# Norm and rotary turn of queries and keys inside the product stage, evictions on ScalarE

## The reference, cut to what matters

```python
def rms_norm(x, g):
    xf = x.astype(jnp.float32)
    y = xf * lax.rsqrt(jnp.mean(xf * xf, axis=-1, keepdims=True) + NORM_EPS)
    return (y * g.astype(jnp.float32)).astype(x.dtype)

def rope_rotate(u, ang):
    u1, u2 = jnp.split(u, 2, axis=-1)
    cs = jnp.cos(ang).astype(u.dtype)
    sn = jnp.sin(ang).astype(u.dtype)
    return jnp.concatenate([u1 * cs - u2 * sn, u2 * cs + u1 * sn], axis=-1)

def axial_rope(x, ang_r, ang_c):
    xr, xc = jnp.split(x, 2, axis=-1)
    ...
    return jnp.concatenate([rope_rotate(xr, ar), rope_rotate(xc, ac)], axis=-1)

def diff_qkv(pq, pk, pv, qn_g, kn_g):
    B, L, _ = pq.shape
    q = rms_norm(pq.reshape(B, L, DIFF_HEADS, 2, DIFF_HEAD_DIM), qn_g)
    k = rms_norm(pk.reshape(B, L, DIFF_HEADS, 2, DIFF_HEAD_DIM), kn_g)
    v = pv.reshape(B, L, DIFF_HEADS, DIFF_V_DIM)
    return q, k, v
```

## Time and profile before

| | before |
|---|---|
| median of 3 runs | 4459.89 us |
| the profiled execution | 4462.74 us, its span 4460.9 us |
| TensorE, VectorE, ScalarE busy | 81%, 38%, 20% of the span |
| product stage of the attention branch | from 682 to 811 us of the span |
| `head_norms` and `rope` stages | 811 to 856 us |
| `transposes` stage | 856 to 864 us |

### The profile page before, as it was taken

One profiled execution on the slowest core, in us unless ns is written; L12 is line 12 of the kernel. 1 busy time (PEld: TensorE's weight loads), 2 busy tenths in 40 slices (PEclk: granted clock), 3 DMA queues, 4 the chain that ended last, 5 costly groups with the idle time before them and its releaser, 6 DMA issues. The chain is left out here.

```text
span 4460.9 us, 68948 instructions
## 1 busy us (share of the span) xinstructions
PE 3593.8 (81%) x29742; PEld 2797.0 (63%) x29742; DVE 1713.9 (38%) x3137; ACT 881.6 (20%) x1426; POOL 58.1 (1%) x74
## 2 busy tenths in 40 slices
PE   4979979579973777747899767999899589778887
PEld 2768968457553433326648557888788555656676
DVE  3645543642232000025444364444300542343433
ACT  2135421132011111111111322111000213221211
POOL 0000000000000000000000000000000000000000
PEclk7979989789985999978899888999999799887888
DMA  5130016113422999963411001444410110112122
GB/s 208 52 120 4 4 50 179 41 46 99 132 85 101 422 422 422 422 239 111 134 43 62 16 10 53 114 113 115 121 52 1 33 36 1 34 57 66 57 76 76
DMA packets 379413, 494.21 MB, mean 111 GB/s; under 512 B 15994, under 2 KB 325787, under 8 KB 370436
## 3 DMA queue, kind: packets, MB, share of 16 engines
q1 hardware_dynamic: 369588, 456.12, 29.4%
q0 software_dynamic: 4432, 25.70, 1.5%
q10 hardware_dynamic: 5120, 8.39, 0.5%
HBM read 458.70 MB, written 31.47 MB: 110 GB/s over the span
## 5 line engine op out<-in xcount | busy, mean ns | idle before, releaser
L288 PE MATMUL banks<-leading,w_rest 128*128 128x512 f32 (+2 forms) x1920 | 726.7, 378 | 128.0 <-DVE w_rest L248 128.0
L288 PE MATMUL banks<-rest,w_leading 128*128 128x512 f32 (+2 forms) x1920 | 714.1, 372 | 0.0
L288 PE MATMUL banks<-leading,w_leading 128*128 128x512 f32 (+2 forms) x1920 | 710.4, 370 | 0.0
L288 PEld LDWEIGHTS banks<-leading,w_rest 128*128 128x128 f32 (+1 forms) x1920 | 380.6, 198 | 201.6 <-issue 85.8
L288 PE MATMUL banks<-w_rest,leading 128*128 128x256 f32 (+3 forms) x1332 | 395.4, 297 | 61.9 <-DVE w_rest L248 61.9
L248 DVE TENSOR_TENSOR w_rest<-land,w_leading 128x1024 fp32r<-128x1024 f32 (+3 forms) x296 | 280.0, 987 | 402.2 <-ACT w_leading L242 402.2
L288 PEld LDWEIGHTS banks<-leading,w_leading 128*128 128x128 f32 (+1 forms) x1920 | 380.2, 198 | 64.1
L288 PEld LDWEIGHTS banks<-rest,w_leading 128*128 128x128 f32 (+1 forms) x1920 | 381.2, 199 | 59.9
L242 ACT CAST w_leading<-land 128x1024 fp32r<-128x1024 f32 (+3 forms) x296 | 239.0, 855 | 779.9 <-DMA land<-in_w_in 314.8
L288 PE MATMUL banks<-w_leading,rest 128*128 128x256 f32 (+3 forms) x1332 | 391.2, 294 | 0.0
L288 PE MATMUL banks<-w_leading,leading 128*128 128x256 f32 (+3 forms) x1332 | 390.8, 293 | 0.0
(11 more groups left out here) (532 smaller groups left out, 4787.5 us busy)
## 6 DMA issues: line engine op xcount, KB each, us to landing
wg<-in_w_exp_gate SPq DMA_DIRECT2D x32, 2048.0 KB, 28.4
wu<-in_w_exp_up SPq DMA_DIRECT2D x32, 2048.0 KB, 28.4
wd<-in_w_exp_down SPq DMA_DIRECT2D x32, 2048.0 KB, 27.9
ws<-in_ada_w SPq DMA_DIRECT2D x96, 512.0 KB, 3.9
land<-in_w_in SPq DMA_DIRECT2D x41, 1024.0 KB, 5.9
land<-in_ffn_up SPq DMA_DIRECT2D x44, 512.0 KB, 5.3
land<-in_ffn_up SPq DMA_DIRECT2D x88, 256.0 KB, 3.3
ws<-in_w_ada SPq DMA_DIRECT2D x32, 512.0 KB, 3.9
```

The lines of the kernel that those rows point to most:

```text
L288: mm = nc.tensor.matmul(bank_of(r, kind, at), lhsT, rhs, start=(k == 0 and q == 0), stop=(k == kt - 1 and q == len(each) - 1))
```

## The change

`products` gets two hooks, `after_dve` and `after_act`, called on VectorE and ScalarE after each result. In the attention branch the evictions go to ScalarE (`nc.scalar.copy`), the banks of the results are 6 in place of 4, and the two stages `head_norms` and `rope` are gone. Their work is done by VectorE in the hook, tile by tile (512 elements per partition), from result 8 on: after results 8 and 9 the squares and sums of the query tiles, two tiles each; at 10 the mean; at 12 the reciprocal; at 12, 14, 16, 18 the two multiplications of the norm, at 13, 15, 17, 19 the turn of the same tile. At 20, 21, 22 the squares and sums of the keys, at 23 the mean, at 25 the reciprocal; at 25 to 30 one key tile each, tiles 0 and 1 (context) with the norm alone, tiles 2 to 5 with norm and turn. ScalarE takes the two square roots after its evictions of results 11 and 24. Squares, sums and swapped halves use the buffer of `qT`, which is free until the transposes.

```diff
--- before.py
+++ after.py
@@ -151,7 +151,7 @@
     m.ahead_next += 1

 
-def products(nc, m, jobs, xT, evac, evac_on, banks=4, kt=KD, wslots=WSLOTS, beside=None, width=512, split=False, k_chunks=1, side=(), pooled=None):
+def products(nc, m, jobs, xT, evac, evac_on, banks=4, kt=KD, wslots=WSLOTS, beside=None, width=512, split=False, k_chunks=1, side=(), pooled=None, after_dve=None, after_act=None):

 

@@ -337,6 +337,16 @@
                     if t:
                         side_add(dve, t - 1)

+            def read_act(act, r, count, j, kind, at):
+                read(act, r, count, j, kind, at)
+                if after_act is not None:
+                    after_act(act, r)
+
+            def read_dve(dve, r, count, j, kind, at):
+                read_both(dve, r, count, j, kind, at)
+                if after_dve is not None:
+                    after_dve(dve, r, read_sem)
+
             def follow(eng, r, count, j, kind, at):
                 if beside is not None:
                     beside(eng, r, j, at, read_sem, aux_sem)
@@ -348,13 +358,13 @@

             @block.scalar
             def _(act):
-                each_result(act, round_weights, read if evac_on == "scalar" else follow)
+                each_result(act, round_weights, read_act if evac_on == "scalar" else follow)

             @block.vector
             def _(dve):
                 if side:
                     nc.vector.tensor_copy(m.cond_wide[:, :, 0:2], side[0][1]).then_inc(spread_sem, 1)
-                each_result(dve, part_weights, read_both)
+                each_result(dve, part_weights, read_dve)
                 if side:
                     side_add(dve, len(side) - 1)

@@ -874,13 +884,87 @@

             def evac(out, j, at, chain):
                 dst = (m.q, m.k, m.v)[j // 2][:, at[0] - (NTC if j < 2 else 0), 256 * (j % 2):256 * (j % 2 + 1)]
-                return nc.vector.tensor_copy(dst, out)
-
-            products(nc, m, jobs, hT_of(m), evac, "vector", split=True, width=256, side=modulation_tiles(m, a, 0, 16, 48))
-            head_norms(nc, m, [(m.q[:].rearrange("p t (n e) -> p (t n) e", e=HD), m.qk_gain[:, 0:HD]),
-                               (m.k[:].rearrange("p t (n e) -> p (t n) e", e=HD), m.qk_gain[:, HD:2 * HD])], HD, EPS)
-            heads = lambda x, t: x[:, t, :].rearrange("p (n e) -> p n e", e=HD)
-            rope(nc, m, [(heads(m.q, t), 8, t) for t in range(NTL)] + [(heads(m.k, NTC + t), 8, t) for t in range(NTL)])
+                return nc.scalar.copy(dst, out)
+
+            heads = lambda x: x.rearrange("p (n e) -> p n e", e=HD)
+            spare = m.qT[:, :, :].rearrange("p a b -> p (a b)")
+            squares, swapped = heads(spare[:, 0:512]), heads(spare[:, 512:1024])
+            sums, roots, rstd = spare[:, 1024:1104], spare[:, 1104:1184], spare[:, 1184:1264]
+            after_q, after_k = 2 * NTL, 2 * NTL + 2 * NT
+            step_sem, summed_sem, rooted_sem = [nc.alloc_semaphore(x) for x in ("qk_step", "qk_summed", "qk_rooted")]
+
+            def after_act(act, r):
+
+                for which, at in ((0, after_q + 3), (1, after_k + 4)):
+                    if r == at:
+                        act.wait_ge(summed_sem, which + 1)
+                        o, n = ((0, 8 * NTL), (8 * NTL, 8 * NT))[which]
+                        nc.scalar.activation(roots[:, o:o + n], sums[:, o:o + n], ACT.Sqrt).then_inc(rooted_sem, 1)
+
+            counted = [0]
+
+            def after_dve(dve, r, read_sem):
+
+                def step(ins):
+                    counted[0] += 1
+                    ins.then_inc(step_sem, 1)
+                    dve.wait_ge(step_sem, counted[0])
+
+                def square_sums(x, t, first):
+                    step(nc.vector.tensor_tensor(squares, heads(x[:, t, :]), heads(x[:, t, :]), ALU.mult))
+                    step(nc.vector.tensor_reduce(sums[:, first + 8 * t:first + 8 * t + 8], squares, AX, ALU.add))
+
+                def mean(first, n):
+                    nc.vector.tensor_scalar(sums[:, first:first + n], sums[:, first:first + n], 1.0 / HD, EPS, ALU.mult, ALU.add).then_inc(summed_sem, 1)
+
+                def inverse(first, n, which):
+                    dve.wait_ge(rooted_sem, which)
+                    step(nc.vector.reciprocal(rstd[:, first:first + n], roots[:, first:first + n]))
+
+                def scale(x, t, first, gain):
+                    h = heads(x[:, t, :])
+                    step(nc.vector.tensor_tensor(h, h, bc(rstd[:, first + 8 * t:first + 8 * t + 8].unsqueeze(2), HD), ALU.mult))
+                    step(nc.vector.tensor_tensor(h, h, gain.unsqueeze(1).to_broadcast([P, 8, HD]), ALU.mult))
+
+                def turn(x, t, row):
+                    h = heads(x[:, t, :])
+                    xv, sw = h.rearrange("p n (a h e) -> p n a h e", a=2, h=2), swapped.rearrange("p n (a h e) -> p n a h e", a=2, h=2)
+                    sn = m.rope_sin[:, row, :].rearrange("p (a h e) -> p a h e", a=2, h=2)
+                    for s in range(2):
+                        step(nc.vector.tensor_tensor(sw[:, :, :, s, :], xv[:, :, :, 1 - s, :], sn[:, :, s, :].unsqueeze(1).to_broadcast([P, 8, 2, 16]), ALU.mult))
+                    step(nc.vector.tensor_tensor(h, h, m.rope_cos[:, row, :].unsqueeze(1).to_broadcast([P, 8, HD]), ALU.mult))
+                    step(nc.vector.tensor_tensor(h, h, swapped, ALU.add))
+
+                n = r - after_q
+                if 0 <= n < 2:
+                    dve.wait_ge(read_sem, after_q)
+                    square_sums(m.q, 2 * n, 0)
+                    square_sums(m.q, 2 * n + 1, 0)
+                if n == 2:
+                    mean(0, 8 * NTL)
+                if n == 4:
+                    inverse(0, 8 * NTL, 1)
+                if 4 <= n < 12 and n % 2 == 0:
+                    scale(m.q, (n - 4) // 2, 0, m.qk_gain[:, 0:HD])
+                if 4 <= n < 12 and n % 2 == 1:
+                    turn(m.q, (n - 4) // 2, (n - 4) // 2)
+                n = r - after_k
+                if 0 <= n < 3:
+                    dve.wait_ge(read_sem, after_k)
+                    square_sums(m.k, 2 * n, 8 * NTL)
+                    square_sums(m.k, 2 * n + 1, 8 * NTL)
+                if n == 3:
+                    mean(8 * NTL, 8 * NT)
+                if n == 5:
+                    inverse(8 * NTL, 8 * NT, 2)
+                if 5 <= n < 5 + NT:
+                    t = n - 5
+                    scale(m.k, t, 8 * NTL, m.qk_gain[:, HD:2 * HD])
+                    if t >= NTC:
+                        turn(m.k, t, t - NTC)
+
+            products(nc, m, jobs, hT_of(m), evac, "scalar", split=True, width=256, side=modulation_tiles(m, a, 0, 16, 48), banks=6,
+                     after_dve=after_dve, after_act=after_act)
             transposes(nc, m, [([m.q[:, t, h * P:(h + 1) * P] for h in range(4)], m.qT[:, :, t * P:(t + 1) * P], None, None) for t in range(NTL)]
                        + [([m.k[:, t, h * P:(h + 1) * P] for h in range(4)], m.kT[:, :, t * P:(t + 1) * P], None, None) for t in range(NT)])
         (m.att,) = buffers(nc, ctx, att=[NTL, 512])
```

## The result

The changed kernel takes 4401.76 us (median of 4 runs, 4393.08 to 4404.5), the kernel before 4459.26 us in the same comparison (4439.4 to 4460.54). The ratio is 0.9878, 95% interval 0.9847 to 0.9909. That is 57.5 us less, where 43.6 us were forecast and 4411 to 4424 us was the range. The profiled execution took 4399.98 us (span 4397.8), against 4462.74 us (span 4460.9): 62.8 us less.

What follows compares the result with a forecast made beforehand. TensorE was taken to bound the product stage and VectorE the norm and turn stages behind it. 44.70 - 1.55 + 0.5 = 43.6 us off 4459.89 gave 4416.3 us, range 4411 to 4424.

Steps and rivals of the forecast that it cites:

- What goes: Between product stage and transposes: the norm and turn stages vanish, so transposes start 44.70 us sooner.
- The lag at result 31: End of product stage: VectorE overruns the rhythm at results 27 to 30, so the stage ends 1.55 us later.
- the lower bound: Lag at result 31: 1.2 us if the addition overlaps its copy, against 2.0 us at the other end.
- Behind the parting: Result 23, after VectorE parts weights: a lag of 1.82 us, gone by result 24.
- TensorE does not wait: Product stage: VectorE may be 2.65 us late, greatest lag 1.82, so TensorE never waits, 0.8 us to spare.
- ScalarE: Product stage: 32 added evictions of 0.37 to 0.42 us, later casts and square roots cost nothing, hidden under matmuls.
- The transposes: Transposes after the product stage: start at the low clock again, perhaps for less long, gaining 0.5 us.
- the most to be gained: First 16 transposes: at most 1.2 us, from 3.65 to the 2.46 us that VectorE's copies need.
- The sum for the place: Product stage to scores: removed stages less the lag plus the transposes' gain, 43.6 us in all.
- The rest of the kernel stays as it is: Outside the changed place: time taken as given, the 43.6 us subtracted from the median of 4459.89 us.
- the bounds that I named: Main forecast's own range: lag 1.2 to 2.0 us, transposes' gain 0 to 1.2, run scatter 1 us.
- more is won behind the stage: Transposes and first scores both run at full clock, another 0.7 and 1.4 us, giving 4414.2 us; chance 0.13.

Runs made afterwards that it cites:

- the work left out: Kernel before with norm and turn of queries and keys left out altogether; 4422.96 us, ratio 0.9924.
- the second: Profile from measuring the changed kernel once more, nothing altered; 4417.95 us over six executions, ratio 0.9911; profiled execution 4431.63 us.
- either pause: Changed kernel with a small stage of two or four unused VectorE fills ahead of the last up-projection; 4421.62 and 4425.76 us.
- the tail was gone: Changed kernel with next weights' casts moved first in the last up-projection and keys' multiplications spread evenly over results; 4353.99 us, ratio 0.9777.
- casts first: Next weights' casts and partings put ahead of each step's first result in the last up-projection; kernel before 4396.89 us, changed kernel 4356.39 us.
- its two variants: Changed kernel with casts first, plus evictions back on VectorE (4352.19 us) or keys' multiplications spread evenly (4353.99 us).

## Why the prediction was wrong

- **What goes, 44.70 us.** Right: 44.83 with the work left out. The release after VectorE's last instruction took 0.79 us in place of 0.92.
- **The lag at result 31, 1.55 us.** Measured 1.20 by the rhythm and 1.27 at the place, near the lower bound. The addition does start before its copy has ended when VectorE is late, which no row of before showed. Behind the parting 1.66 in place of 1.82.
- **TensorE does not wait.** Right: no wait in the stage but the last one of 1.38 us. The dearer small instructions cost nothing.
- **ScalarE.** Right: 0.37 us an eviction, no table load, casts in time.
- **The transposes, +0.5 us.** Wrong in sign in the first profile: to the first score it took 0.68 us longer. In the second, and with either pause, it took 0.26 us less (8.42). I had counted on the shorter idle time ahead of them; they started at the low clock all the same (3.65 and 3.27 us for the first 16). The 1.2 us that I had called the most to be gained came only where the tail was gone as well: 7.45 us, 1.23 less than before.
- **The sum for the place.** 43.6 forecast, 43.15 in the first profile, 43.9 in the second. That it comes so near is in part luck: the lag was sized 0.3 us too high and the transposes 1.2 or 0.2 us too well.
- **The rest of the kernel stays as it is.** This is the step that failed. I subtracted the local sum from the median of three runs that agreed within 2 us and took the other 4.2 ms as given; my own range held 1 us for what the runs scatter, on the word of those three, and the bounds that I named give 4414.2 to 4418.2 us, not the 4414.5 to 4419 that I wrote. The runs showed 20.5 us between the two profiled executions in a stage that the change does not touch, the last up-projection. Three alike executions were a chance draw: 43 executions of the same kernel span 35 us, ten of the changed one 40. The changed kernel's first four were from its faster part. The profile had the signs: the 2.85 us waits for `w_rest`, and a granted clock of 0.80 in that stage, of which none of my rows was. The rival "more is won behind the stage" had the right kind of cause, a clock that falls or not, but looked for it only in the stages next to the change, at 2 us and not at 20.

What is shown: the local gain, that the late stage's length varies with the time at 1.2 GHz in either kernel, and that with the shorter wait the two kernels differ by 40.5 us. What stays open: why the clock falls behind a wait of 2.85 us in one tile and not in the next, and whether the changed kernel's late stage is, over many executions, as long as that of the kernel before. The pooled medians are 50 us apart, the means 44.9, against 43 to 44 at the place; ten executions cannot settle a difference of a few microseconds.

The fastest kernels here are those with casts first; the changed kernel with it takes 0.9773 of the time before, and its two variants lie within 5 us of it.

## What to carry to other kernels

Work of one engine that stands in a stage of its own can be put beside a stage that another engine bounds; its price is then not its duration but its excess over the rhythm, per result, and only the excess that is left at the end reaches the time. Before a local sum is set against a whole time, look for stages elsewhere that wait a few microseconds in every round and whose mean granted clock lies between its two levels: here one added or took 20 us whatever was changed. To value the change itself, compare the same instructions in the two traces, from a point behind which they run alike, or mend that stage in both kernels first.

## What the hardware showed that I had not expected

- The same matmuls behind the same 2.85 us wait ran at 0.63 or at 0.40 us each from tile to tile and execution to execution; 125.9 us at 1.2 GHz in one execution, 57.6 in another, 143.0 in a third of the same kernel as the second. The stage took 362.7, 342.2 and 369.5 us.
- A change of order that took this wait from 2.85 us to mostly 1.5 us brought the clock to 1.00 behind the first 5 us and the stage from 362.7 to 291.8 us, 71 us, of which the waits themselves are the smaller part: from its first matmul on TensorE waited 59.1 us for `w_rest` in the stage before and 32.1 us with the edit. The wait in the kernel before with the edit:

```profile
4052.60 0.51 PE L288 MATMUL banks<-leading,w_rest 128*128 128x512 f32 x1 [1.50 <-DVE w_rest L248]
4052.95 0.40 PE L288 MATMUL banks<-rest,w_leading 128*128 128x512 f32 x1
```

- When VectorE is late, an addition on it starts 0.20 us after a copy of 0.29 us has started (797.31, 797.51); when the copy itself starts as soon as its matmuls are done, 0.28 us (805.78, 806.06 in the kernel before).
